# Rates with tokens in partitions, and a level's four product steps placed between its two products

## The reference, cut to what matters

```python
proj = h @ w_in
a_in = proj[..., o0 + GDN_VALUE_DIM:o0 + GDN_VALUE_DIM + GDN_HEADS]     # 8 columns
b_in = proj[..., o0 + GDN_VALUE_DIM + GDN_HEADS:]                       # 8 columns
beta = sigmoid(b_in)
g = -exp(a_log) * softplus(a_in + dt_bias)
g_cum = cumsum(g)                            # within a chunk
decay = exp(where(tril, g_cum[:, None] - g_cum[None, :], -inf))
L = strict_lower((k * beta) @ k.T * decay);  A = L + I
u = solve(A, v * beta);  w = solve(A, k * beta * exp(g_cum))
```

## Time and profile before

| | us |
|---|---|
| median of three runs | 2624.92 (2624.57 to 2629.37) |
| profiled execution, its own time | 2623.83 |
| its span | 2622.0 |
| TensorE busy | 2410.0 (92%) |
| VectorE busy | 1123.8 (43%) |
| ScalarE busy | 903.0 (34%) |
| GpSimd busy | 357.3 (14%) |

### The profile page before, as it was taken

The page is one execution under the profiler, slowest core; times in us unless marked ns, Lnnn a source line. Parts: engine busy times, 40 slices in busy tenths (PEclk is TensorE's granted clock), DMA queues, the critical chain, the costliest instruction groups (busy, mean ns, idle before and its releaser), DMA issues.

```text
span 2622.0 us, 30221 instructions
## 1 busy us (share of the span) xinstructions
PE 2410.0 (92%) x12144; PEld 1890.2 (72%) x12144; DVE 1123.8 (43%) x1186; ACT 903.0 (34%) x1086; POOL 357.3 (14%) x164
## 2 busy tenths in 40 slices
PE   7899999989999978889999998999987798999997
PEld 4577877768888755567888886777765586788886
DVE  3757654552332455444332235342256524433234
ACT  4445553432312344433232224333233422422122
POOL 0246574357600000000000000000000000000000
PEclk9899999989999988899999999999998799999999
DMA  6233432335422313222222223111210022222222
GB/s 268 82 129 121 153 121 85 124 129 178 175 86 90 112 60 117 80 80 81 96 86 100 87 96 117 65 64 64 96 48 32 30 83 80 81 96 96 96 80 96
DMA packets 38435, 259.80 MB, mean 99 GB/s; under 512 B 4280, under 2 KB 4536, under 8 KB 8144
## 3 DMA queue, kind: packets, MB, share of 16 engines
...
...
## 4 chain that ended last, share of the span: by engine, by line
PE 73%; issue 9%; POOL 8%; DVE 5%; ACT 3%; DMA 1%; SPq 0%; POOLq 0%; DVEq 0%; ACTq 0%
PE D L268 18%; PE D L269 18%; PE D L270 18%; POOL adar L325 4%; POOL adar L323 3%; PE D L283 3%; PE D L284 3%; PE D L285 3%; DMA fw<-in_ada 1%; PE D L1527 1%; PE D L304 1%; PE D L305 1%; PE D L303 1%; ACT hi L312 1%; PE D L1543 1%
## 5 line engine op out<-in xcount | busy, mean ns | idle before, releaser
L316 DVE TENSOR_TENSOR lo<-raw,hi 128x2048 fp32r<-128x2048 f32 (+1 forms) x185 | 423.8, 2291 | 460.7 <-ACT hi L312 460.5
L268 PE MATMUL D<-hH,lo 128*128 128x512 f32 x1456 | 585.5, 402 | 0.0
L269 PE MATMUL D<-hL,hi 128*128 128x512 f32 x1456 | 575.3, 395 | 0.0
L270 PE MATMUL D<-hH,hi 128*128 128x512 f32 x1456 | 575.0, 395 | 0.0
L312 ACT ACTIVATE hi<-raw 128x2048 fp32r<-128x2048 f32 (+1 forms) x185 | 342.9, 1853 | 498.5 <-PE D L270 285.3
L268 PEld LDWEIGHTS D<-hH,lo 128*128 128x128 f32 x1456 | 274.9, 189 | 70.6 <-issue 8.0
L269 PEld LDWEIGHTS D<-hL,hi 128*128 128x128 f32 x1456 | 275.0, 189 | 66.7 <-issue 4.0
L270 PEld LDWEIGHTS D<-hH,hi 128*128 128x128 f32 x1456 | 274.5, 189 | 65.2
L325 POOL TENSOR_TENSOR adar<-adar 128x1024 f32<-128x1024 f32 (+2 forms) x120 | 201.8, 1682 | 9.4
L323 POOL TENSOR_TENSOR adar<-adar,cact 128x2048 f32<-128x2048 f32 x40 | 155.6, 3889 | 347.5 <-DMA adar<-in_ada 237.6
L269 PE MATMUL D<-aL,hi 128*128 128x512 f32 x444 | 176.0, 396 | 0.0
...
## 6 DMA issues: line engine op xcount, KB each, us to landing
...
```

The source lines that it names most:

```text
L268: T_.matmul(o, lo[s.slot][:, w], H[:, k, :], start=(k == 0), stop=False)
L269: T_.matmul(o, hi[s.slot][:, w], L[:, k, :], start=False, stop=False)
L270: last = T_.matmul(o, hi[s.slot][:, w], H[:, k, :], start=False, stop=(k == kc - 1))
L316: V_.tensor_tensor(lo[s.slot][:, 0:n], raw[s.slot][:, 0:n], hi[s.slot][:, 0:n], ALU.subtract).then_inc(lo_ready, 1)
```

## The change

Four edits. (1) The rates are made with tokens in partitions: slab 0 is the moving operand, 16 columns of it, and the activations are the weights, so 4 token tiles x 8 k x 3 = 96 matmuls of 16 columns (rates_pe); the arithmetic runs on 128 partitions x 32; the cumulative sum is a matmul with a triangle of ones (rates_pe_2); three transposes and one copy make rows for the broadcasts. One small matmul ahead of the first norm spreads dt_bias and a_log. (2) The order before pair 0 is another one on three engines: the same 48 steps are spread over seven fills, and conv, silu, square and Ln of k's first head come ahead of those of the second. (3) A level issues fill(2 * lv_fill) ahead of its second products and none behind. (4) `gated(0, m)` of pair 3 moves ahead of split_lo and level 2, and the second sum of squares at the end of pairs 0 to 2 moves between the two Gram matrices of the next pair. In the diff the bodies that are replaced (rows_dve_1 to rows_dve_4, tsc_dve) are left out; they stand above.

```diff
@@ -183,8 +183,11 @@
 egl = sb("egl", [P, 2, NT], scope=gdn)
 go = sb("go", [P, KC, T], scope=gdn)
 lvl = sb("lvl", [P, 7 * P], i32, gdn)
-rows, rtmp = go[0:GH, 0:4, :], go[0:GH, 4:7, :]
-bcast = nc.dram_tensor("bcast", (3 * GH, T), fp32, kind="Internal").ap()
+tk = go[:, 0, :].rearrange("p (a t h) -> p a t h", t=NT, h=GH)
+tri = go[:, 1, 0:P]
+rowb = go[0:NT * GH, 2, 0:3 * P]
+diag, hcol = small[0:GH, 16:32], small[:, 32:48]
+bcast = nc.dram_tensor("bcast", (3 * NT * GH, P), fp32, kind="Internal").ap()
 gdn.close()
 ffn = ExitStack()
@@ -359,6 +362,8 @@
 def first_cols_pe(pe, g, h):
     pe.wait_ge(row_ready, 2 * g + h + 1)
+    if g == 3:
+        pe.wait_ge(gg["hcol"], 1)
     for m in range(2):
         last = T_.matmul(first_bank[g][:, 2 * h + m:2 * h + m + 1], arow[:, 2 * h + m, :], ones[:, 0:1],
                          start=True, stop=True)
@@ -625,80 +630,119 @@
 unit_bank = lambda s, m: D[0 if s == K_SEQ(0) else 1][:, m, :]
...
+AB_BANK = (D[0][:, 0, 0:2 * GH], D[0][:, 1, 0:2 * GH], D[2][:, 0, 0:2 * GH], D[3][:, 1, 0:2 * GH])
+a_, b_, u_, w_, ln_, dl_, eq_, g_, eg_, df_ = (tk[:, k] for k in range(10))
+over_t = lambda c: hcol[:, c:c + GH].unsqueeze(1).to_broadcast([P, NT, GH])
+def heads_dve(dve, chain):
+    chain.link(V_.tensor_scalar(diag[:, 0:GH], ident[0:GH, 0:GH], vec[0:GH, V["dt_b"]:V["dt_b"] + 1], None, ALU.mult))
+    dve.wait_ge(gg["row"], 1)
+    V_.tensor_scalar(diag[:, GH:2 * GH], ident[0:GH, 0:GH], small[0:GH, 0:1], -1.0, ALU.mult,
+                     ALU.mult).then_inc(gg["head"], 1)
+    dve.wait_ge(gg["head"], 2)
+    V_.tensor_copy(hcol, W[:, 0:2 * GH]).then_inc(gg["hcol"], 1)
+def heads_pe(pe):
+    pe.wait_ge(gg["head"], 1)
+    T_.matmul(W[:, 0:2 * GH], ones[0:GH], diag, start=True, stop=True).then_inc(gg["head"], 1)
+def rates_pe(pe, ready):
+    s = Slab(G_AB)
+    pe.wait_ge(lo_ready, s.plus(1))
+    pe.wait_ge(rms_ready, 1)
+    cols = lambda t_, k: t_[s.slot].rearrange("p (k j n) -> p k j n", k=KC, j=2)[:, k, :, 0:GH]
+    for k in range(KC):
+        ready(k)
+        for t in range(NT):
+            tok = slice(t * P, t * P + P)
+            T_.matmul(AB_BANK[t], hL[:, k, tok], cols(hi, k), start=(k == 0), stop=False)
+            T_.matmul(AB_BANK[t], hH[:, k, tok], cols(lo, k), start=False, stop=False)
+            last = T_.matmul(AB_BANK[t], hH[:, k, tok], cols(hi, k), start=False, stop=(k == KC - 1))
+    last.then_inc(slab_done, 1)
+def rates_dve_1(dve, chain):
     L = chain.link
...
     dve.wait_ge(slab_done, 1)
...
+    V_.tensor_scalar(tri, neg, -1.0, None, ALU.is_ge)
+    for t in range(NT):
+        V_.tensor_tensor(a_[:, t], AB_BANK[t][:, 0:GH], hcol[:, 0:GH], ALU.add)
+        last = V_.tensor_copy(b_[:, t], AB_BANK[t][:, GH:2 * GH])
+    last.then_inc(bank_free[0], 1)
+    dve.wait_ge(bank_free[0], 1)
+    V_.scalar_tensor_tensor(out=u_, in0=a_, scalar=-1.0, in1=a_, op0=ALU.mult, op1=ALU.max).then_inc(gg["rowd"], 1)
+def rates_dve_2(dve, chain):
     L = chain.link
...
     dve.wait_ge(gg["row"], 2)
     L(V_.tensor_scalar(w_, u_, 1.0, None, ALU.add))
...
+    V_.tensor_scalar(dl_, w_, 1.0, None, ALU.subtract).then_inc(gg["rowd"], 1)
+    dve.wait_ge(gg["rowd"], 2)
+    L(V_.tensor_scalar(eq_, dl_, 0.0, None, ALU.is_equal))
+    L(V_.tensor_tensor(dl_, dl_, eq_, ALU.add))
+    L(V_.reciprocal(dl_, dl_))
     dve.wait_ge(gg["row"], 3)
...
+    L(V_.tensor_tensor(ln_, ln_, eq_, ALU.add))
+    L(V_.tensor_tensor(ln_, ln_, u_, ALU.mult))
+    L(V_.tensor_tensor(ln_, ln_, dl_, ALU.mult))
+    L(V_.scalar_tensor_tensor(out=ln_, in0=a_, scalar=0.0, in1=ln_, op0=ALU.max, op1=ALU.add))
+    V_.tensor_tensor(g_, ln_, over_t(GH), ALU.mult).then_inc(gg["rowd"], 1)
+def rates_pe_2(pe):
+    pe.wait_ge(gg["rowd"], 3)
+    T_.matmul(W[:, 0:NT * GH], tri, g_.rearrange("p t h -> p (t h)"), start=True, stop=True)
+    T_.matmul(W[:, NT * GH:2 * NT * GH], ones, g_.rearrange("p t h -> p (t h)"), start=True,
+              stop=True).then_inc(gg["rowp"], 1)
+def rates_dve_3(dve):
     dve.wait_ge(gg["rowp"], 1)
...
+    V_.tensor_copy(tsc[:, 0].rearrange("p t h -> p (t h)"), W[:, 0:NT * GH]).then_inc(gg["rowd"], 1)
+    dve.wait_ge(gg["rowd"], 4)
+    V_.tensor_tensor(df_.rearrange("p t h -> p (t h)"), W[:, NT * GH:2 * NT * GH],
+                     tsc[:, 0].rearrange("p t h -> p (t h)"), ALU.subtract).then_inc(gg["rowd"], 1)
+    dve.wait_ge(gg["row"], 6)
+    V_.scalar_tensor_tensor(out=tsc[:, 3], in0=tsc[:, 1], scalar=-1.0, in1=eg_, op0=ALU.mult,
+                            op1=ALU.mult).then_inc(gg["tsc"], 1)
 def rows_pe(pe):
...
+    pe.wait_ge(gg["row"], 5)
+    pe.wait_ge(gg["rowd"], 5)
+    for a, src in enumerate((tsc[:, 0], tsc[:, 1], eg_)):
+        last = T_.transpose(W[0:NT * GH, a * P:a * P + P], src.rearrange("p t h -> p (t h)"), ident)
     last.then_inc(gg["rowp"], 1)
+def rows_dve(dve):
+    dve.wait_ge(gg["rowp"], 2)
+    V_.tensor_copy(rowb, W[0:NT * GH, 0:3 * P]).then_inc(gg["tsc"], 1)
+def rates_act(act):
+    act.wait_ge(gg["rowd"], 1)
+    S_.preload_act_table_set("natural_log_exp_and_others")
+    S_.activation(u_, u_, ACT.Exp, scale=-1.0).then_inc(gg["row"], 1)
+    act.wait_ge(gg["rowd"], 2)
+    S_.activation(ln_, w_, ACT.Ln).then_inc(gg["row"], 1)
+    act.wait_ge(gg["rowd"], 4)
+    S_.activation(eg_, tsc[:, 0], ACT.Exp).then_inc(gg["row"], 1)
+    S_.activation(tsc[:, 1], b_, ACT.Sigmoid).then_inc(gg["row"], 1)
+    act.wait_ge(gg["rowd"], 5)
+    S_.activation(tsc[:, 2], df_, ACT.Exp).then_inc(gg["row"], 1)
 def rows_out(sp):
...
+    sp.wait_ge(gg["tsc"], 2)
+    for a in range(3):
+        sp.dma_start(bcast[a * NT * GH:(a + 1) * NT * GH, :],
+                     rowb[:, a * P:a * P + P]).then_inc(gg["row_out"], 16)
     sp.wait_ge(gg["row_out"], 48)
 def row_in(sp, dst, kind, x, done):
     for m in range(2):
...
+        src = bcast.rearrange("(k t h) n -> k h t n", k=3, t=NT)[kind, 2 * x + m]
+        sp.dma_start(half_t(dst, m), src.unsqueeze(0).to_broadcast([P, NT, P])).then_inc(gg[done], 16)
 def gdn_act(act):
@@ -729,35 +773,24 @@
     nle = lambda: S_.preload_act_table_set("natural_log_exp_and_others")
-    u_, w_ = rtmp[:, 1, :], rtmp[:, 2, :]
-    gc, beta, dl = (rows[:, k, :] for k in range(3))
-    S_.activation(small[0:GH, 0:1], vec[0:GH, V["a_log"]:V["a_log"] + 1], ACT.Exp)
     split_hi(act, Slab(2))
-    act.wait_ge(bank_free[0], 1)
-    S_.activation(u_, u_, ACT.Exp, scale=-1.0).then_inc(gg["row"], 1)
-    S_.activation(beta, beta, ACT.Sigmoid).then_inc(gg["row"], 1)
-    nle()
-    w("rowd", 1)
-    S_.activation(gc, gc, ACT.Ln).then_inc(gg["row"], 1)
+    rates_act(act)
     for m in range(2):
         silu(qs[0], 1, m)
     for m in range(2):
         square_unit(qs[0], fs, m, m + 1)
     split_hi(act, Slab(3))
-    nle()
-    w("rowd", 2)
-    S_.activation(w_, gc, ACT.Exp).then_inc(gg["row"], 1)
-    S_.activation(dl, u_, ACT.Exp).then_inc(gg["row"], 1)
-    for m in range(2):
-        silu(ks, 2, m)
-    for m in range(2):
-        square_unit(ks, xi, m, m + 3)
-    split_hi(act, Slab(4))
+    silu(ks, 2, 0)
+    square_unit(ks, xi, 0, 3)
     nle()
     for m in range(2):
         log_unit(fs, m, m + 1)
     exp_pair(fs, 2)
     decay(0)
+    split_hi(act, Slab(4))
+    silu(ks, 2, 1)
+    square_unit(ks, xi, 1, 4)
+    nle()
     for m in range(2):
         log_unit(xi, m, m + 3)
     exp_pair(xi, 4)
@@ -984,22 +1017,21 @@
         V_.tensor_tensor(ks[:], ks[:], (fs if x else xi)[:], ALU.mult).then_inc(gg["kn"], 1)
-    rows_dve_1(dve, chain)
+    rates_dve_1(dve, chain)
+    rates_dve_2(dve, chain)
     split_lo(dve, Slab(2))
-    rows_dve_2(dve, chain)
+    rates_dve_3(dve)
+    rows_dve(dve)
     for m in range(2):
         conv(qs[0], 0, 0, 1, m)
     split_lo(dve, Slab(3))
-    rows_dve_3(dve, chain)
-    rows_dve_4(dve)
-    for m in range(2):
-        conv(ks, 1, 0, 2, m)
-    tsc_dve(dve)
+    conv(ks, 1, 0, 2, 0)
+    gaps(0)
+    q_norm(0)
     split_lo(dve, Slab(4))
-    gaps(0)
+    conv(ks, 1, 0, 2, 1)
+    beta_decay(0)
     conv(vs, 2, 0, 3, 0)
-    q_norm(0)
-    beta_decay(0)
     k_norm(0)
     dve.wait_ge(lvl_in, 16)
@@ -1107,13 +1139,13 @@
             k_norm(1)
             conv(qs[0], 0, 2, Q_SEQ(2), 0)
             continue
+        if not front:
+            gated(0, 0)
+            gated(0, 1)
         split_lo(dve, Slab(6 + 3 * p))
         level(2)
         if front:
             conv(ks, 1, x, K_SEQ(x), 0)
-        else:
-            gated(0, 0)
-            gated(0, 1)
         v_turned(0)
         level(3)
         v_turned(1)
@@ -1200,17 +1232,23 @@
         w("fsq", n)
         T_.matmul(W, ones, f_[:, m, :], start=True, stop=True).then_inc(gg["ssq"], 1)
-    fill(44)
+    fill(8)
+    rates_pe_2(pe)
+    fill(4)
     rows_pe(pe)
+    fill(16)
+    w("tsc", 2)
+    sum_squares(fs, 0, 1)
     fill(4)
-    w("tsc", 1)
-    sum_squares(fs, 0, 1)
     w("fln", 1)
     sum_squares(fs, 1, 2)
+    fill(6)
     w("fln", 2)
     sum_squares(xi, 0, 3)
+    fill(5)
     w("fln", 3)
     sum_squares(xi, 1, 4)
```

(84 more changed lines are left out.)

8 lines of the change are left out of this document (removed).

## The result

The changed kernel takes 2639.2 us (median of 6 runs, 2634.91 to 2645.18) against 2627.14 for the kernel before (6 runs); the ratio is 1.0047, 95% interval 1.0031 to 1.0063. The forecast was 2621.7 with a range up to 2632: it failed, and on the side of its rival "the clock stays low", whose time was 2628.8.

What follows compares the result with a forecast made beforehand. TensorE was taken to wait for VectorE and ScalarE before pair 0 and in small pieces within the pairs. Terms -4.1 + 7.2 - 4.4 - 1.9 = -3.2 us gave a median of 2621.7 us, range 2611 to 2632.

Steps and rivals of the forecast that it cites:

- the clock stays low: Rival, slab 0's product: 16-column matmuls do not raise the clock, product ends at 61, +7.1 us, 2628.8; chance 0.25.
- (1): Product of slab 0: 96 small matmuls, half clock until 46 us, end at 54.9 instead of 54.75: +0.1 us.
- (2): Stretch before pair 0: shorter chain, -2.1 us, and Gram and transposes at full clock, -2.1; -4.1 with the product's +0.1.
- (3): Levels of the pairs: first products wait for mask copies, work queued on VectorE comes late; +7.2 us, bounds 0 to +11.
- the rest: Remaining case: half-clock spells behind new waits of 2 us, +1.5 us each; chance 0.05.
- levels are cheap: Rival on the levels: their term is about 0 since VectorE is never late; 2614.5 us, chance 0.28.
- (4): Moved sum of squares between Gram halves: -2.6 us at one pair, -0.9 at two others; -4.4, bounds -5 to -3.
- (5): Gate multiplications moved out of level 2 of pair 3: -1.9 us, bounds -3.4 to 0.

Runs made afterwards that it cites:

- warm: Changed kernel plus 16 matmuls of 512 columns, results thrown away, ahead of the 96 small ones; ratio 1.0081 to the kernel before.
- the two light kernels: Changed kernel, and it with level steps on both sides of second products again, both with GpSimd's modulation work cut to 16 of 256 columns; ratios 0.9961 and 0.9924.
- levels_split: Changed kernel with a level's four product steps back on both sides of its second products; ratio 1.0007 to the kernel before, 2631.5 us.
- rates_only: Changed kernel with levels, second sum of squares and gate multiplications as before, keeping rates, order before pair 0 and broadcasts; ratio 1.0017 to the kernel before.
- best1: Changed kernel with slab 0's columns packed and stationary (24 matmuls), level steps, second sum and gate multiplications back in place; ratio 0.9964 to before, 2624.3 us.
- packed_no_sum: Changed kernel with slab 0's columns packed and stationary, level steps and second sum back in place, gate multiplications still moved; ratio 0.9950 to before, 2615.8 us.
- packed_split: Changed kernel with slab 0's columns packed and stationary, level steps back on both sides, second sum and gate still moved; ratio 0.9945 to before, 2614.1 us.
- the second trace: Profile of the changed kernel run once more, unedited, beside the kernel before; ratio 1.0041, pair 0 took 116.3 us.

## Why the prediction was wrong, point by point

**(1) The product of slab 0: the step that failed.** "The clock is half until 46 us ... then 74 x 0.12": the price of a small matmul at half clock was right (0.20 taken, 0.213 measured), but all 96 paid it. I carried over the instant at which the kernel before got its full clock, though the work up to that instant was what the edit replaced. End 62.4 instead of 54.9; the upper bound of 61 was low by 0.013 us a matmul (1.3) and by a start at 41.86 instead of 41.4. The rival's numbers (61, +7.1) fit nearly (62.4, +7.5), and its 0.25 was too little: "single-column matmuls ran between others at full pace" told only that they don't end a full clock at once. `warm` is the run that shows the mechanism.

**(2) The stretch before pair 0 was right,** a little better than forecast: 54.3 us from product's end to q by k, 5.2 less than before where 4.2 had been worked out. The chain's points came 0 to 1 us from where the working put them. In the timeline of VectorE the last product of g, the last of the factors in `tsc` and the copy to rows:

```profile
68.25 0.19 DVE L691 TENSOR_TENSOR go<-go,small 128x32 f32<-128x32 f32 x1
...
74.36 0.19 DVE L706 SCALAR_TENSOR_TENSOR tsc<-tsc,go 128x32 f32<-128x32 f32 x1 [3.15 <-ACT tsc L731]
74.47 0.54 DVE L718 COPY go<-D 32x384 f32<-32x384 f32 x1
```

The first ends 6.1 us and the last 12.6 us behind 62.4, against 5.7 and 12.3; the two convs end at 18.7 (18.5), the first Ln at 30.8 (30.8) and k_norm at 51.5 (51.8). Gram started at 114.49, outside the 104 to 111 that I had named, by (1) alone.

**(3) Levels: mechanism right, size probably too small,** 7.2 taken, about 10 measured (3.4 to 4.0 per mille, uncertain by 2; 10.1 us between the profiles of the two light kernels). The 0.36 bare microseconds of a plain level, the v transposes at 1.82 and 1.81 us and, in pair 3, 1.15 at step 225 and 2.06 at step 241 all stand in the trace. The last ones:

```profile
420.09 0.50 PE L1207 MATMUL D<-hH,lo 128*128 128x512 f32 x1 [1.15 <-DVE lo L319]
...
441.31 4.48 DVE L319 TENSOR_TENSOR lo<-raw,hi 128x2048 fp32r<-128x2048 f32 x1
...
445.84 0.62 PE L1207 MATMUL D<-hH,lo 128*128 128x512 f32 x1 [2.06 <-DVE lo L319]
```

What the term lacked: half clock behind such a wait (the window from 446.1 to 449.5 us has a granted clock of 0.50), which I had put among "the rest" with 0.05 (1.6 us more in the levels of a pair 1 or 2 where such a spell fell); a split before step 241 that GpSimd drew out to 4.48 us where I had 3.36; and pair 0, for which I had let GpSimd's wait absorb everything: without GpSimd it is 2.4 us, and with it no profile pair can tell, since pair 0 scatters by 10. The rival "levels are cheap" is out.

**(4) The moved sum: -4.4 expected, about nothing found.** Its tails came, -0.5 and -0.9 in pairs 1 and 2. But Gram now comes sooner, and the next thing that TensorE waits for, the first mask copy, did not. In this execution the stretch from q by k to the first level is 1.6 us longer at pair 1 and 2.2 at pair 3; 1.3 and 0.8 of these are the longer wait for the copy, and behind the one of pair 3 the clock was at half (0.50 from 401.7 to 405.1 us). I had asked what stands behind Gram on TensorE and not what VectorE does there with GpSimd beside it. The -2.6 at pair 0 can't be read off: pair 0 changes by 10 us between executions of the same kernel.

**(5) The gate: -1.9 expected;** with split levels it is worth 3.0 in the profiles of levels_split and rates_only (51.35 against 54.38) and 2.3 in best1 and packed_no_sum. In the changed kernel the waits of (3) stand where it gained, and no run parts the two.

In sum, as a ledger of kernels: (1) and (2) +2.1 to +2.4 instead of -4.1; (3) +10 instead of +7.2; (4) and (5) -3 to -5 instead of -6.3, by the ratios of rates_only to levels_split and of best1 to packed_split. That is +7 to +9 where -3.2 was forecast; measured were 12.1, with an interval of 8 to 16.5. Each difference of ratios in this ledger is itself uncertain by 2 to 3 per mille, so it agrees with the measurement without proving the shares. The largest miss, (1), rests on the trace and not on ratios: 7.5 us in the product alone.

**What stays open.** The lot of (4) at pair 0; why GpSimd and VectorE meet as they do in one execution and not in the next (TensorE of the second trace is 0.7 us behind the first through pair 0 until 182.3 to 185.6 us, where its clock is 0.50 and the first one's full; then comes a split of 4.74 us instead of 2.41); and what TensorE has to do for its clock to stay full.
